# A hybrid diffusion step with PEER experts: TensorE's expert sums one group behind, from the second merge to the keys

## What is computed

```
h = rmsnorm(x, norm1_g) * (1 + sc1) + sh1
# four mixers on h: Fourier, convolution, attention, window attention
merged = gates[0]*y_f + gates[1]*y_c + gates[2]*y_a + gates[3]*y_w
x = x + g1 * (merged @ w_out)
h = rmsnorm(x, norm2_g) * (1 + sc2) + sh2
# experts: for each token 8 heads, each picks 16 of 16384 experts
sc = einsum("chpd,pkd->chpk", q, subkeys)        # 2 x 128 scores a head
s_half, i_half = top_k(sc, 16)                   # then the best 16 of 16 x 16 pairs
gate = softmax(top_s)
act = gelu(einsum("chkd,cd->chk", u_tab[eidx], h))
x = x + g2 * einsum("chk,chkd->cd", gate * act, v_tab[eidx])
```

## Time and profile before

| | |
|---|---|
| median of three runs | 5485.01 us (5474.55 to 5494.79) |
| profiled execution | 5502.59 us |
| its span | 5500.8 us |
| TensorE matmul busy | 4392.1 us (80%) |
| VectorE busy | 3596.6 us (65%) |
| ScalarE busy | 1252.1 us (23%) |
| GpSimd busy | 1542.8 us (28%) |
| gathers, share of 16 DMA engines | 61.7% (1342.26 MB) |
| all other loads and stores | 12.3% (244.21 MB) |
| chain that ended last | TensorE 40%, DMA 27%, VectorE 21% |

### The profile page before, as it was taken

One profiled execution on the slowest core, in us unless ns is written; L12 is line 12 of the kernel. 1 busy time (PEld: TensorE's weight loads), 2 busy tenths in 40 slices (PEclk: granted clock), 3 DMA queues, 4 the chain that ended last, 5 costly groups with the idle time before them and its releaser, 6 DMA issues.

```text
span 5500.8 us, 45164 instructions
## 1 busy us (share of the span) xinstructions
PE 4392.1 (80%) x13844; PEld 2483.3 (45%) x13844; DVE 3596.6 (65%) x7876; ACT 1252.1 (23%) x3024; POOL 1542.8 (28%) x1290
## 2 busy tenths in 40 slices
PE   7989999978878676666689899898898776666665
PEld 5846764444444222222267478544445442222222
DVE  1932177766667988876638312886676589888765
ACT  1132147611111111111111311565111111111111
POOL 0000013223331454455400000232233324454453
PEclk9989999989989888888889799999899898888887
DMA  4133458779986999999921334687899869999997
GB/s 166 61 129 134 142 206 313 281 284 348 354 340 227 368 419 421 422 421 422 379 98 54 121 115 139 244 313 268 298 360 354 325 230 393 421 421 421 421 422 302
DMA packets 227570, 1589.36 MB, mean 289 GB/s; under 512 B 26112, under 2 KB 28416, under 8 KB 47872
## 3 DMA queue, kind: packets, MB, share of 16 engines
q0 software_dynamic: 184320, 1342.26, 61.7%
q1 hardware_dynamic: 43008, 244.21, 12.3%
HBM read 1581.66 MB, written 4.72 MB: 288 GB/s over the span
## 4 chain that ended last, share of the span: by engine, by line
PE 40%; DMA 27%; DVE 21%; ACT 4%; issue 4%; DVEq 2%; POOL 1%; SPq 0%; POOLq 0%; ACTq 0%
DMA B<-tables,R 19%; PE ps L529 9%; PE ps L539 7%; DVE B L1561 6%; PE ps L681 5%; DMA A<-tables,R 4%; PE ps L586 4%; DVE A L1595 4%; PE ps L546 3%; PE ps L667 3%; DMA H<-tables,R 2%; PE ps L559 2%; DVE A L1561 2%; DMA B<-ws 1%; DVE H L1561 1%
## 5 line engine op out<-in xcount | busy, mean ns | idle before, releaser
L529 PE MATMUL ps<-B,R 128*128 128x512 f32 x2264 | 1267.0, 707 | 516.8 <-ACT R L970 515.8
L495 POOL DMA_INDIRECT B<-tables,R x788 | 933.0, 1184 | 2124.4 <-PE ps L529 978.8
L1561 DVE SCALAR_TENSOR_TENSOR B<-B,M 128x1024 f32<-128x1024 f32 x788 | 947.8, 1223 | 287.8 <-DMA B<-tables,R 269.8
L529 PEld LDWEIGHTS ps<-B,R 128*128 128x128 f32 x2264 | 485.5, 225 | 1201.7 <-ACT R L970 628.9
L539 PE MATMUL ps<-H,B 128*128 128x384 f32 (+1 forms) x2048 | 593.8, 444 | 21.6 <-DMA B<-ws 20.7
L529 PE MATMUL ps<-A,R 128*128 128x512 f32 x736 | 414.5, 705 | 187.5 <-ACT R L970 187.5
L495 POOL DMA_INDIRECT A<-tables,R x282 | 339.4, 1203 | 635.3 <-PE ps L529 440.0
L539 PEld LDWEIGHTS ps<-H,B 128*128 128x128 f32 x2048 | 400.6, 196 | 221.1 <-issue 56.7
L964 ACT ACTIVATE T<-T 128x2 f32<-128x2 f32 (+1 forms) x452 | 93.3, 206 | 1620.3 <-DVEq L1563 1618.9
L970 ACT ACTIVATE R<-cs,A 128x128 f32<-128x128 f32 x898 | 309.6, 395 | 588.7 <-DVEq L1584 588.7
L529 PE MATMUL ps<-H,R 128*128 128x512 f32 x544 | 315.8, 723 | 142.1 <-ACT R L970 142.1
(11 more groups left out here) (237 smaller groups left out, 5050.5 us busy)
## 6 DMA issues: line engine op xcount, KB each, us to landing
B<-ws SPq DMA_DIRECT2D x120, 1024.0 KB, 5.2
B<-ws SPq DMA_DIRECT2D x128, 768.0 KB, 4.4
B<-tables,R POOLq DMA_INDIRECT x788, 13.2
A<-tables,R POOLq DMA_INDIRECT x282, 13.6
R<-tabs SPq DMA_DIRECT2D x2, 2176.0 KB, 14.5
H<-tables,R POOLq DMA_INDIRECT x194, 11.2
x<-xin SPq DMA_DIRECT2D x1, 2560.0 KB, 9.2
y<-M SPq DMA_DIRECT2D x1, 2560.0 KB, 7.9
```

What stands on the lines that cost most here:

```text
L495: pool.indirect_dma_start(out=ring[s], out_offset=None, in_=tables[:, :], in_offset=bass.IndirectOffsetOnAxis(ap=EI[:, n:n + 1], axis=0),) ...
L529: mm = pe.matmul(ps[:, bk + c, :], diag[PE_AT[n] % DIAGS], v_row[:, c * 512:(c + 1) * 512], start=(n in PE_FIRST), stop=(PE_AT[n] + 1 == P ...
L1561: v.scalar_tensor_tensor(out=u_row, in0=u_row, scalar=1.0, in1=h2[:, g.tile, :], op0=ALU.mult, op1=ALU.mult, accum_out=dots[:, o:o + 1])
```

## The change

Three edits. First, from the merge to the key scores TensorE sums the group before the one that VectorE weighs in the same step: every call `experts(l, q)` becomes `experts(l, q - 1)`, the call ahead of the merge goes, and the last loop starts one group earlier. Second, the four first merge weights of chunk 1 all wait for the same count, that of the first, so that they begin together. Third, in `weighed` the weights come ahead of the selection part.

```diff
-                    sp.wait_ge(w_used.sem, used(l, n) if n in range(BLOCKS, BLOCKS + WS) else
+                    sp.wait_ge(w_used.sem, used(l, BLOCKS) if n in range(BLOCKS, BLOCKS + WS) else
                                used(l, AT_OP + AGAIN) if n in range(AT_OP + AGAIN, AT_OP + AGAIN + WS) else nth(l, n) + 1)
...
                 values(TILES - 1, TILES - 2, 1, 1)
-                experts(l, AT_MERGE - 1)
                 pe.wait_ge(a_on.sem, a_on.at(l, 4 * TILES))
                 for s in range(N_MG):
                     mix_gates(l, 1, s)
...
                     mix_branch(l, 1, s)
                     for q in range(*MG_GROUPS[s]):
-                        experts(l, q)
+                        experts(l, q - 1)
                 pe.wait_ge(mg_m.sem, mg_m.at(l, 2 * KD))
                 for i in range(len(CHUNKS[1])):
                     for part in range(4):
                         out_part(l, 1, i, part)
-                        experts(l, AT_OUT + i * OUT_STEP + part)
+                        experts(l, AT_OUT + i * OUT_STEP + part - 1)
                 for i, t in enumerate(CHUNKS[1]):
-                    experts(l, AT_NORM + i)
+                    experts(l, AT_NORM + i - 1)
                     norm_transposes(l, t, TILES + t, XSc[1][i % 2], i % 2 * 2, TILES + t - 2 if i >= 2 else None)
                 for i in range(len(CHUNKS[1])):
                     row_transposes(l, 1, i)
-                    experts(l, AT_ROWS + i)
+                    experts(l, AT_ROWS + i - 1)
...
                     if hp in KEY_GROUPS:
-                        experts(l, AT_KEYS + KEY_GROUPS.index(hp))
+                        experts(l, AT_KEYS + KEY_GROUPS.index(hp) - 1)
                 key_scores(l, 1, UNITS - 1)
 
-                for q in range(AT_END, N_GROUPS):
+                for q in range(AT_END - 1, N_GROUPS):
                     experts(l, q)
...
                     if g.place in OPENS[g.tile]:
                         gates(g)
+                    weights(q)
                     if q in SELECT:
                         select(*SELECT[q])
-                    weights(q)
```

## The result

The changed kernel takes 5394.56 us, the median of four runs (5386.24 to 5399.98), against 5489.02 for the kernel before in the same session: a ratio of 0.9833 [0.9818, 0.9847], so 94 us fewer. Forecast were 5387 us and 98 us fewer. The profiled execution's span is 5392.7 us, 108.1 less than before.

A forecast was written before the change was run, and what follows sets the result against it. The ceiling was TensorE's 106.3 us a layer of waits for diagonals and merge weights, ahead of a DMA-filled gather stream. Terms +2 - 18 - 8 - 3 - 14 - 8 = -49, twice -98: 5485 - 98 = 5387 us, range 5300 to 5470.

The forecast's parts named there:

- Norm and row transposes: Second norm and row transposes: sums run while ScalarE modulates, pace 5.2 us; -14 us a layer, bounds -19 and 0.
- Queries and keys: Stage of queries and key scores: 5 us from three first rounds, 3 from later waits; -8 us a layer, bounds 0 and -21.5.
- which sets the pace and gains its own wait, 29.9/16 = 1.9 us at most: First key rounds: TensorE sets the pace and gains only its own wait, 3 rounds, 5 us.
- Attention: Attention stage: loads begun together +4, weights ahead of selection 0, slots freed in the last groups -2; +2 us a layer.
- 17 x 0.6 - 10 = 0: Attention, 34 groups: new gelu waits in one group in three cancel the 10 us of waits that stop; 0.
- Merge beside selection: First 10 merge groups: two thirds of VectorE's 27.4 us gelu wait go, weight waits included; -18 us a layer.
- Rest of the merge: Last 38 merge groups: -22 from TensorE's idling, +13 for ring slots held longer; taken as -8 us a layer.
- The bound of -22: Rest of the merge: at a DMA share of 0.99 it would still take 255 us, so at most 22 go.
- the one of the ring slots: Rival: slots held longer make the merge wait for gathers, +31 us a layer, 5547 us; chance 0.10.
- VectorE binds at once: Rival: merge -6, norm -10, keys -4, attention +8, rest 0; -12 us a layer, 5461 us; chance 0.20.
- Every wait of TensorE is won: Rival: all 106.3 us a layer of TensorE's waits are gained, 213 us in all, 5272 us; chance 0.10.
- Below 40 us: Sign to look for: TensorE's wait for diagonals between merge and keys falls below 40 us a layer.

The follow-up runs named there:

- e4: Kernel before, with TensorE summing one group behind only in the stage of queries and keys; 5462.90 us, ratio 0.9947.
- e9: Changed kernel with all three edits, plus in odd merge steps the first group's sum ahead of the branch products; 5366.67 us, ratio 0.9779.
- e2: Kernel before, with only the four merge weight loads begun together; 5478.53 us, ratio 0.9985.
- e3: Kernel before, with only the weights put ahead of the selection parts; 5475.64 us, ratio 0.9977.
- e1: Kernel before, with only the sums one group behind from merge to keys; loads and order of weights as before; 5390.88 us, ratio 0.9824.
- e6: e5 with the weights ahead of selection only from group 54 on; 5387.98 us, ratio 0.9823.
- e7: e6 with, in odd merge steps, the first group's sum ahead of the branch products; 5357.18 us, ratio 0.9770.
- e8: e6 without the sums one group behind in groups 61 to 98; 5394.46 us, ratio 0.9830.
- e10: e7 with the moved sum put ahead of the gate products too, where it stood before the change; 5395.33 us, ratio 0.9824.
- e11: e7 with its order in even steps too, which moves only the last attention group's sum; 5361.55 us, ratio 0.9762.
- e5: Changed kernel with weights behind selection again and the second to fourth load held until slot 99 is summed; 5385.64 us, ratio 0.9818.
- e12: e1 with e7's order, so without the edits to loads and weights; 5382.52 us, ratio 0.9810.

## Why the prediction was right

The total was right to 8 us. By the medians a layer gained 47 us where 49 were forecast; the table's first line sums to -52, some 7 of them from the one execution of the kernel before. The mechanism was right, TensorE's waits going and a price in the ring coming, but that the sum is so close is in part luck: the keys brought 12 us more than forecast, the attention cost 4 to 6 more, the merge beside selection brought 5 less and the output 3 less, and these errors cancel.

- **Norm and row transposes, -14, measured -13.5.** Right, and for the reason given. In the timeline after, from 1576 to 1606, a sum of 3.53 us now lies beside ScalarE's eight activations, where in the earlier trace rows it stood ahead of them, and from transposes to transposes it is 5.12 us (1581.34 to 1586.46), where I had 5.2:

```profile
1581.34 1.97 PE L512 MATMUL ps<-cs,B 128*128 128x128 f32 x8 [4.99 <-DVE B L1211]
...
1583.10 3.53 PE L529 MATMUL ps<-B,R 128*128 128x512 f32 x4
1583.34 2.90 ACT L909 ACTIVATE H<-ps,aff 128x128 f32<-128x128 f32 x8 [2.74 <-PE ps L512]
...
1586.46 1.04 PE L512 MATMUL ps<-cs,B 128*128 128x128 f32 x8
...
1605.98 5.32 PE L586 MATMUL ps<-H,B 128*128 128x384 f32 x16
```

  VectorE's gelu waits in the stretch, 18.5 us in 5 places before, are 0.7 after.

- **Queries and keys, -8, measured -20.** The step that failed is "which sets the pace and gains its own wait, 29.9/16 = 1.9 us at most". Which wait ends last stood in the trace of before: ScalarE copies the queries (line 952) ahead of the gelu, and that copy waits for TensorE. First before, then after, both in the first key round:

```profile
1648.49 0.48 ACT L952 COPY A<-ps 128x384 f32<-128x384 f32 x1 [8.93 <-PE ps L586]
1648.87 0.21 ACT L964 ACTIVATE T<-T 128x2 f32<-128x2 f32 x1
```

```profile
1611.35 0.48 ACT L951 COPY A<-ps 128x384 f32<-128x384 f32 x1 [1.29 <-PE ps L586]
...
1614.39 0.20 ACT L963 ACTIVATE T<-T 128x2 f32<-128x2 f32 x1 [2.57 <-DVEq L1562]
```

  Gelu waited for the queries; now it waits for VectorE's own products. For that TensorE has to enter the stage ahead: its first queries start at 1605.98, 4.6 us ahead of the first key group's products (1610.6), where before they started 3.7 us behind them (1642.87 against 1639.2). The difference, 8.3 us, is the lag's work in norm and rows. In e4, where this start is missing, the first rounds gain the 5 that I priced; with it they gain 12. The other rounds gain 8 in all three cases, not 3: VectorE's gelu waits there, 5.2 us, and one of 2.0 for the gate's part on ScalarE, are all gone. What I took as the far bound, VectorE's 21.5 us of the earlier trace rows, was the answer within 2 us.

- **Attention, +2, measured +8.5.** That is this profile; e9, with the same program there, has +3.1, and the mean of the four layers is +5.8. Alone the loads cost 4.3 us (e2; I charged 4) and the weights order nothing (-0.1 in e3, for -2). The failed step is "17 x 0.6 - 10 = 0", right in its sum and not in its parts. In groups 0 to 16 the weights order costs 5.1 and 5.0 us (after), 4.1 and 3.9 (e3), 3.4 and 1.4 (e9), and 0.7 and 0.6 in e1, which hasn't it. VectorE's gelu waits there went from 2.1 us in 4 places to 6.2 in 7 (751.5 to 877, after): those that selection covered are longer than I had them, and more of them came than went. In e3 groups 45 to 50 give 2.5 and 3.7 us back; with the loads beside it they don't (+4.1 and +0.7 in after, +3.3 and -0.8 in e9). The loads alone cost +4.5 and +2.2 there (e2), 3.4 in the mean, where I charged 4; the same groups of e6, e7, e8, e10 and e11, with late loads, spread from -2.9 to +2.2. The bound set in the prediction (attention up by over 10) is touched in layer 0 of after with 10.5, and in none of the other three layers. The Trainium skill, "DMA: Bandwidth & Descriptors", "Queues, rings and completion order", has each DMA engine take turns between queue rows, and the estimate by that rule was 2.5 us. No run here decides between it and my 4: e2's mean lies between them, and so does the growth of the longest wait for one gather, 2.9 us (5.47 to 8.41).

- **Merge beside selection, -18, measured -13.** VectorE's gelu wait fell by 16.8 us (27.4 to 10.6), close to my two thirds. Two things took a part back: its wait for gathers rose from 6.0 to 9.9 us, and TensorE now waits 6.7 us for gate rows. That the weight waits lie "inside these 18" was right: the lag alone gains 10, the loads alone 11, the two together 11 (e5), all three edits 13. In e7, where the merge's ring is no longer held up, the same stretch gives -18.4.

- **Rest of the merge, -8, measured -14; output, -3, measured 0.** Half of the -14 belongs to the two profiled executions: before takes 276.2 us in the mean of its layers where all twelve layers with its order have 271.0, and after 262.2 where the eight with its order have 264.1. That makes -7, near what I charged. The direction of each part was right, gelu waits going and gather waits coming, and so was the size of the ring's price. From the product's start to the end of its sum the one TensorE slot of a period is held 8.9 us before and 10.1 after in layer 0, 9.0 and 9.5 in layer 1 (means of ten slots of groups 64 to 95): +1.2 and +0.5, against the 1 that I charged, and not 3.5 or 7.98. What I left out is the other kind: the TensorE slot of the group behind it is held 6.8 us in place of 11.5. GpSimd's waits for the two releases in layer 0 (places B and A, before, then after) show the same, the first 1.3 us a period longer, the second almost gone:

```profile
POOL A L495 <- PE ps L529: 83.3, 13, 8.2
POOL B L495 <- PE ps L529: 17.8, 12, 4.8
```

```profile
POOL B L495 <- PE ps L529: 34.1, 13, 3.9
POOL A L495 <- PE ps L529: 8.6, 8, 3.1
```

  The bound of -22 was none: e7 gains 27.7 in layer 0. It rested on the DMA share: 0.91 of 277.7 are 253 us of busy queues. e7 moves the same bytes (384 GB/s x 250.0 us = 96.0 MB; 347 x 277.7 = 96.4 before) in 0.97 x 250.0 = 243 us of them.

Of the rivals, the one of the ring slots had the mechanism and the wrong size: VectorE does wait for gathers after (51.2 us), and e7 and e9 show what the order is worth, 28 to 31 us of the whole. But its turning point, 3.2 us a period, is never reached, as the slot is held only 1.2 longer. "VectorE binds at once" is refuted by the keys. "Every wait of TensorE is won" fell with the 55.0 us that TensorE still waits; the 18.5 us of them in the keys (6 places) stand beside a VectorE that waits 0.6 us for gelu, so they cost next to nothing. "Below 40 us" was the wrong sign to look for: an engine that is no longer the bound may wait.

That three edits were made and one pays is the experiments' finding, not the prediction's: lag 0.9824 [0.9801, 0.9846], all three 0.9833 [0.9818, 0.9847], loads or weights by themselves 0.15 to 0.23%. Beside the lag they gain 3 us a layer beside selection and lose 9 in the attention (3 in e9's profile). Once the order is put right they do count: e12 without them is at 0.9810 [0.9791, 0.9830], e9 with them at 0.9779 [0.9766, 0.9793], e7, with the loads late and the weights order from group 54 on, at 0.9770 [0.9757, 0.9783]. Which of the two counts no run separates; e12's waits for weights point to the loads.

Open: whether the late third load is all that e12 loses in the stretch beside selection against e1 (104 against 98.5 us); its weight waits are 13.5 us against 8.1, but no run changed that load alone. And which part of the merge's gain in e7 is the clock's: the granted clock there rises from 0.95 to 1.00, and a matmul of that stretch takes 234.38/681 = 0.344 us in place of 251.41/704 = 0.357. No run held the one without the other.

## What to carry to other kernels

When one engine is let run a step behind, ask of every buffer that it releases when that release now comes, and move only that release forward: between two products here (e7) it wins 0.5% more, ahead of both (e10) all of it is lost again. Read the price from the engine that waits for the release (GpSimd here), not from the time between product and sum alone, which is shorter in e10 than in e7. To price a removed wait, follow who waits for whom to the engine that stands ahead in the order of a third one (the query copy ahead of gelu), and count the lead that an engine brings from the stage before, not only the waits inside the stage. Try the edits of a bundle singly: two of three added nothing here to the first until the order was put right. And hold a stage against more than one execution: here two single ones made up half of one stage's gain.

## What was not expected of the hardware

The DMA share of a stretch is no measure of work that is left to do: the same 96 MB took 253 us of it before and 243 in e7, in a stretch that was 28 us shorter, at 384 in place of 347 GB/s. And four loads of 0.75 MB begun together land in a median of 8.3 us (1062 to 1128 us, after), one alone in 4.2 (1062 to 1117, before), with the gathers beside them at 7.8 in place of 6.4:

```profile
B<-ws SPq DMA_DIRECT2D x4, 768.0 KB, 8.3
B<-tables,R POOLq DMA_INDIRECT x9, 7.8
```

```profile
B<-ws SPq DMA_DIRECT2D x1, 768.0 KB, 4.2
B<-tables,R POOLq DMA_INDIRECT x9, 6.4
```
